# The first RMS norm's tokens laid out feature first: sums through a product with ones, a late chunk, and the S5 parameters on GpSimd

## What is computed

```python
def _rms_norm(x, g):
    y = x * lax.rsqrt(jnp.mean(x * x, axis=-1, keepdims=True) + EPS)
    return y * g

def _prologue(x, ctx, c, c_ctx, g, w_mod, b_mod):
    sh, sc, gt = _ada(c, w_mod, b_mod)            # silu(c) @ w_mod + b_mod, in three parts
    shc, scc, gtc = _ada(c_ctx, w_mod, b_mod)
    hx = _rms_norm(x, g) * (1 + sc[:, None]) + sh[:, None]
    hc = _rms_norm(ctx, g) * (1 + scc) + shc
    return jnp.concatenate([hc, hx], axis=1), ...

def _even_layer(...):
    u, v, g_a, xs, g_b = split(h @ w_in)          # five parts of width 512
    y_a = _chunk_gmlp(u, v, ...) * silu(g_a)      # layer norm of v, 128-token chunks
    y_b = _s5_bidir(xs, lam, log_dt, b, c, ...) * silu(g_b)   # diagonal state space model, both directions
    x = x + gt * (concat(y_a, y_b) @ w_out)

def _s5_discretize(lam_re, lam_im, log_dt, b_re, b_im):
    dt = jnp.exp(log_dt)
    mag = jnp.exp(lam_re * dt)
    lb = mag * (cos(lam_im * dt), sin(lam_im * dt))
    f = (lb - 1) / lam                            # complex; den = lam_re^2 + lam_im^2
    bb = f * b
```

## Time and profile before

| | |
|---|---|
| median of 3 runs | 1305.07 us (1303.98 to 1305.39) |
| profiled execution | 1301.15 us |
| its span, first to last instruction | 1299.3 us |
| mean granted TensorE clock | 0.992 |
| TensorE busy | 1223.0 us, 94% |
| VectorE, ScalarE, GpSimd busy | 851.6, 518.3, 445.6 us |
| HBM read and written | 95.71 and 30.93 MB |

### The profile page before, as it was taken

How to read it: one execution, slowest core, us unless ns; L and a number is a source line. 1 busy time by engine, 2 the same in 40 slices (tenths; PEclk the granted TensorE clock), 3 DMA queues, 4 the chain that set the end, 5 groups by cost and what they waited for, 6 DMA issues and landing times.

```text
span 1299.3 us, 21119 instructions
## 1 busy us (share of the span) xinstructions
PE 1223.0 (94%) x8508; PEld 1079.1 (83%) x8508; DVE 851.6 (66%) x1494; ACT 518.3 (40%) x956; POOL 445.6 (34%) x358
## 2 busy tenths in 40 slices
PE   1799989999999899999999999999999999999997
PEld 1789878888888848999999998877788888888997
DVE  6697956989925253136484899448877877776125
ACT  6632353320015331034524432146666666665012
POOL 0600000000000003332112212139999888988332
PEclk9899999999999999999999999999999999999999
DMA  9614677425422962103211112330000000000402
GB/s 347 241 66 130 153 209 247 148 81 203 162 90 85 324 231 56 64 33 116 70 44 34 33 66 81 111 100 9 9 17 9 17 9 17 17 9 9 162 28 103
DMA packets 87408, 127.99 MB, mean 99 GB/s; under 512 B 12912, under 2 KB 59376, under 8 KB 86512
## 3 DMA queue, kind: packets, MB, share of 16 engines
q1 hardware_dynamic: 77200, 110.81, 25.8%
q10 hardware_dynamic: 10112, 15.85, 3.5%
HBM read 95.71 MB, written 30.93 MB: 97 GB/s over the span
## 4 chain that ended last, share of the span: by engine, by line
PE 78%; DVE 11%; DMA 4%; ACT 3%; POOL 3%; issue 2%; SPq 0%; ACTq 0%; POOLq 0%; DVEq 0%
PE ps L1732 10%; PE ps L1734 10%; PE ps L1733 10%; PE ps L1743 5%; PE ps L1744 5%; PE ps L1745 5%; PE ps L1986 3%; DVE region_d L1008 3%; PE ps L2020 2%; PE ps L2021 2%; PE ps L2022 2%; PE ps L2006 2%; PE ps L2009 2%; PE ps L2008 2%; PE ps L2007 2%; PE ps L1598 2%
## 5 line engine op out<-in xcount | busy, mean ns | idle before, releaser
L1732 PE MATMUL ps<-w_hi,a_hi 128*128 128x256 f32 x896 | 256.6, 286 | 9.9 <-DVE b_lo L1109 6.3
L1733 PE MATMUL ps<-w_lo,a_hi 128*128 128x256 f32 x896 | 254.9, 284 | 0.0
L1734 PE MATMUL ps<-w_hi,c_lo 128*128 128x256 f32 x736 | 208.2, 283 | 0.0
L601 POOL TENSOR_TENSOR region_b<-region_b,region_d 128x256 f32<-128x256 f32 x40 | 29.7, 749 | 510.0 <-DVE region_d L1412 510.0
L1732 PEld LDWEIGHTS ps<-w_hi,a_hi 128*128 128x128 f32 x896 | 173.2, 193 | 12.2 <-issue 3.7
L1733 PEld LDWEIGHTS ps<-w_lo,a_hi 128*128 128x128 f32 x896 | 173.4, 194 | 0.0
L594 POOL TENSOR_TENSOR w_lo<-weight_ring,w_hi 128x2048 fp32r<-128x2048 f32 x16 | 74.0, 4625 | 199.3 <-ACT w_hi L649 199.3
L1734 PEld LDWEIGHTS ps<-w_hi,c_lo 128*128 128x128 f32 x736 | 141.2, 192 | 0.0
L1743 PE MATMUL ps<-a_hi,w_hi 128*128 128x512 f32 (+1 forms) x384 | 138.6, 361 | 1.4 <-ACT region_d L649 1.4
L1508 DVE TENSOR_REDUCE small<-ps 128x1 f32<-128x1280 f32 x64 | 95.2, 1487 | 65.1 <-PE ps L1986 65.1
L1744 PE MATMUL ps<-b_lo,w_hi 128*128 128x512 f32 (+1 forms) x384 | 136.6, 356 | 0.0
(11 more groups left out here) (225 smaller groups left out, 2940.9 us busy)
## 6 DMA issues: line engine op xcount, KB each, us to landing
weight_ring<-in_w_mod SPq DMA_DIRECT2D x10, 2048.0 KB, 8.5
weight_ring<-in_we_in SPq DMA_DIRECT2D x10, 1024.0 KB, 6.0
weight_ring<-in_wo_in SPq DMA_DIRECT2D x10, 1024.0 KB, 5.2
weight_ring<-cop_t_scratch SPq DMA_DIRECT2D x4, 1536.0 KB, 7.9
region_a<-in_x SPq DMA_DIRECT2D x4, 1024.0 KB, 14.4
region_c<-in_w_mod SPq DMA_DIRECT2D x2, 2048.0 KB, 19.3
bop_scratch<-region_d ACTq DMA_DIRECT2D x16, 256.0 KB, 2.6
cop_t_scratch<-region_d SPq DMA_DIRECT2D x8, 512.0 KB, 7.4
```

Source lines behind the costliest of these rows:

```text
L1732: te.matmul(o, th, wh[:, k], start=k == 0, stop=False)
L1733: te.matmul(o, th, wl[:, k], start=False, stop=False)
L1734: last = te.matmul(o, tl, wh[:, k], start=False, stop=k == last_k)
```

## The change

- The host lays the tokens out feature first as well (`xt`). SP loads its first 768 tokens (chunks 0 and 1) in two halves of four slabs into `hT0`. The other 512 (chunk 2) come after the fourth modulation slab, feature first into `hT0` and token first into `XQ`.
- Sums of squares of the first 768: ScalarE squares four slabs in one instruction, VectorE adds two slabs to the other two, TensorE multiplies what is left by a matrix of ones, so each partition has all 768 sums. ScalarE takes 768 roots on every partition, VectorE refines the reciprocals there, and multiplies slabs 0 to 3 by them (`scaled`). Slabs 4 to 7 get it together with their scale (`gained`, `gained_rest`, `gained_round`).
- Chunk 2: ScalarE squares and sums four token tiles, one root, `row_rstd`; TensorE spreads the four columns by transposes (`rstd_across`, listed as "bc" after v tile 1), ScalarE copies them to `rstd_rows`.
- The 80 transposes, their copies and the scalings of tiles are gone. The mods(2) product moves behind v's first two token tiles; weight half 1 of v on slabs 0 to 3 comes ahead of slabs 4 to 7.
- The lists after v and after xs change: bop(4), lags, xs weights, gb weights and vg stand one or two places later. VectorE's evacuation of the sixth modulation slab moves behind build_bl(2), and w_lo of xs ahead of build_cl(0).
- The exponentials, the sine and the signs go from VectorE to GpSimd, in float arithmetic (rounding by adding and subtracting 12582912). VectorE keeps 1 / den.
- The S5 arrays b and c are loaded by SP after the tokens, not by ScalarE at the start.

The orders written out by hand:

```diff
-        early = [(M[0], 0), (M[1], 1), (("v", 0), 2), (("v", 1), 0), (M[4], 1), (M[5], 1), (("xs", 0), 1), (("xs", 1), 0),
+        early = [(M[0], 0), (("v", 0), 2), (M[1], 1), (("v", 1), 0), (M[4], 1), (M[5], 1), (("xs", 0), 1), (("xs", 1), 0),
...
-        after_v = {1: [("mods", 4)], 2: [("cols", 4)], 5: [("mods", 5)], 6: [("cols", 5), ("xs", 0)], 7: [("bop", 0)], 8: [("bop", 4)],
-                   9: [("lags", 0)]}
-        after_xs = {0: [("xs", 1)], 2: [("bop", 8)], 4: [("ws", 0)], 5: [("lags", 1)], 6: [("gb", 0), ("bop", 12)], 7: [("vg", 0)],
-                    8: [("vg", 5)]}
+        after_v = {1: [("bc", 2)], 2: [("mods", 4)], 3: [("cols", 4)], 5: [("mods", 5)], 6: [("cols", 5)], 7: [("xs", 0), ("bop", 0)],
+                   9: [("bop", 4)]}
+        after_xs = {1: [("xs", 1)], 2: [("lags", 0)], 4: [("bop", 8)], 5: [("ws", 0)], 7: [("lags", 1)], 8: [("gb", 0), ("bop", 12)],
+                    9: [("vg", 0)], 10: [("vg", 5)]}
```

SP:

```diff
-            token_loads(X, ld_x)
-            ring_load(*M[0])
-            ring_load(*M[1])
-            ring_load("v", 0)
+            for e in range(2):
+                sp.dma_start(hT0[:, 4 * e:4 * e + 4, 0:T01], xt[:, 4 * e:4 * e + 4, 0:T01]).then_inc(ld_x[e], 16)
+            ring_load(*M[0])
+            ring_load("v", 0)
+            ring_load(*M[1])
+            off_ring_load(2, s_ld_v)
             ring_load("v", 1)
+            off_ring_load(3, s_ld_ws)
+            sp.dma_start(hT0[:, :, T01:TOK], xt[:, :, T01:TOK]).then_inc(ld_x[2], 16)
+            for i in range(4):
+                c = T01 - NCTX + P * i
+                sp.dma_start(XQ[:, 2 * i:2 * i + 2, T01:TOK],
+                             x[0, c:c + P, :].rearrange("p (a f) -> p a f", a=2)).then_inc(ld_x[3 + i // 2], 16)
+            sp.dma_start(braw.rearrange("p r g h -> p (r g h)"), b_in).then_inc(s_ld_b, 16)
+            sp.dma_start(Cx.rearrange("p r g h -> p (r g h)"), c_in).then_inc(s_ld_b, 16)
```

ScalarE:

```diff
+            for e in range(2):
+                act.wait_ge(ld_x[e], 16)
+                a.activation(XQ[:, 4 * e:4 * e + 4, 0:T01], hT0[:, 4 * e:4 * e + 4, 0:T01], ACT.Square).then_inc(s_sq, 1)
+            act.wait_ge(s_ss_mm, 1)
+            act.wait_ge(s_consts, 2)
+            a.activation(rstd_rows[:, 0:T01], sums, ACT.Sqrt, bias=epsc, scale=1.0 / D).then_inc(s_rt, 1)
+            weights_round(("v", 0))
+            mod_row(0)
             mod_row(1)
+            h_round(0)
+            h_round(1)
             mod_row(2)
+            weights_round(("v", 1))
             mod_row(3)
+            gained_round(0, range(4, KT), 0)
+            gained_round(1, range(4, KT), 4)
+            for t in range(6, TT):
+                act.wait_ge(ld_x[t // 2], 32)
+                i = 2 * t - 12
+                z = XQ[:, i:i + 2, T01:TOK]
+                a.activation(z, z, ACT.Square, accum_out=ssq[:, t:t + 1]).then_inc(s_sq, 1)
+            act.wait_ge(s_sq, 6)
+            a.activation(rstd[:, 6:TT], ssq[:, 6:TT], ACT.Sqrt, bias=epsc, scale=1.0 / D).then_inc(s_rt, 1)
+            act.wait_ge(s_bc_mm, 1)
+            copy(rstd_rows[:, T01:TOK], ps[:, 7, :]).then_inc(s_bc_ok, 1)
+            gained_round(2, range(KT), 8)
```

VectorE:

```diff
+            for e in range(2):
+                dve.wait_ge(s_sq, e + 1)
+                z = XQ[:, 4 * e:4 * e + 2, 0:T01]
+                v.tensor_tensor(z, z, XQ[:, 4 * e + 2:4 * e + 4, 0:T01], ALU.add).then_inc(s_pre, 1)
+            dve.wait_ge(s_rt, 1)
+            rows = rstd_rows[:, 0:T01]
+            ts(rows_m, sums, 1.0 / D, ALU.mult, EPS, ALU.add)
+            refined(rows_t, rows_m, rows)
+            scaled(0)
+            scaled(1)
+            weights_rest(("v", 0))
             half_evac(0)
+            h_rest(0)
+            h_rest(1)
+            weights_rest(("v", 1))
             half_evac(1)
+            gained(0, range(4, KT))
+            gained_rest(0, range(4, KT), 8)
+            gained(1, range(4, KT))
+            gained_rest(1, range(4, KT), 12)
+            dve.wait_ge(s_rt, 2)
+            row_rstd(slice(6, TT))
+            v.tensor_copy(small[:, 335:336], small[:, 0:1]).then_inc(s_rs0, 1)
+            dve.wait_ge(s_bc_ok, 1)
+            for e in range(2):
+                gained(2, range(4 * e, 4 * e + 4))
+                gained_rest(2, range(4 * e, 4 * e + 4), 16 + 4 * e)
...
             build_bl(1)
-            mod_evac(0, 6, 16, 24)
+            weights_rest(("xs", 0))
             build_cl(0)
-            weights_rest(("xs", 0))
...
             weights_rest(("xs", 1))
+            mod_evac(0, 6, 16, 24)
             k_diagonal(0)
```

TensorE:

```diff
+            def rstd_across():
+
+                pe.wait_ge(s_rs0, 1)
+                pe.wait_ge(s_mod_ev, 2)
+                for i in range(4):
+                    last = tr(ps[:, 7, P * i:P * i + P], rstd[:, 6 + i:7 + i].broadcast_to([P, P]))
+                last.then_inc(s_bc_mm, 1)
+
+            for e in range(2):
+                pe.wait_ge(s_pre, e + 1)
+                for k in range(4 * e, 4 * e + 2):
+                    te.matmul(sums[:, 0:256], ones_f, XQ[:, k, 0:256], start=k == 0, stop=k == 5)
+                    last = te.matmul(sums[:, 256:T01], ones_f, XQ[:, k, 256:T01], start=k == 0, stop=k == 5)
+            last.then_inc(s_ss_mm, 1)
             mods(0)
             mod_cols(0)
-            to_features(0, *x0)
             mods(1)
             mod_cols(1)
-            to_features(1, *x0)
-            mods(2)
-            mod_cols(2)
...
+            ws = [split_of(("v", 0))]
             for t in range(6):
                 if t == 2:
-                    to_features(2, *x0)
+                    mods(2)
+                    mod_cols(2)
+                for k in range(4):
+                    if t in (0, 2):
+                        pe.wait_ge(s_h_lod, k + 1 if t == 0 else k + 5)
+                    v_part(ws[0], t, 0, (k,))
+            ws.append(split_of(("v", 1)))
+            for t in range(6):
+                if t == 2:
                     mods(3)
+                if t == 3:
                     mod_cols(3)
+                v_part(ws[1], t, 1, range(4))
             for t in range(TT):
+                if t in (0, 2, 6):
+                    pe.wait_ge(s_h_lod, {0: 12, 2: 16, 6: 24}[t])
                 if t >= 6:
                     pe.wait_ge(s_v_ev, t - 5 if t < 8 else t - 1)
+                ks = range(4 if t < 6 else 0, KT)
+                v_part(ws[0], t, 0, ks)
+                v_part(ws[1], t, 1, ks).then_inc(s_v_mm, 1)
                 between_tiles(after_v.get(t, ()))
```

302 lines of the change are left out of this document (134 added, 168 removed).

## The result

The changed kernel takes 1309.01 us (median of 6, 1307.67 to 1311.44), the kernel before beside it 1304.13: a ratio of 1.0041, 95% interval 1.0026 to 1.0055. Timed again on another chip it was 1.0036 (1.0021 to 1.0050). It is slower by some 5 us, where the forecast was 1304.1 and the range ended at 1309.0. The profiled execution took 1309.46, its span is 1307.7, 8.4 more than before's. Two further profiles of the kernel before (one with an input that nobody reads) have spans of 1302.4 and 1301.9, so its first was a short one; three further ones of the changed kernel (one with its inputs in another order) have 1304.0, 1302.9 and 1301.9, so its first was a long one.

The account below looks back on a forecast made before the run. TensorE, busy 94%, was taken to bound the kernel. Its first product comes 8.6 us earlier, but S 5.7 later delays CL(1) and ScalarE sets gating at 203.2 against 204.20: -1.0 us, 1304.1, range 1297 to 1309.

Parts of the forecast that it names:

- What bounds: Whole kernel: TensorE, busy 94% of a 1299.3 us span, so a change in front pays only where TensorE still waits.
- the new front: Start to the first product with tokens: TensorE starts it at 40.4, not 48.99, 8.6 us earlier.
- The v stage: TensorE waits 4.2 us for the late chunk's rstd, yet is through v at 118.8, some 8 us earlier.
- S: End of VectorE's work on h, ahead of its first BB pass: 85.8 against 80.08, 5.7 us later.
- 16 passes of 0.62: VectorE's last passes on h, after the late chunk's transposes and copy: 16 at 0.62 us each, ending at S.
- Where that goes: Chain after v: CL(0) at 126.2 (before 124.6), xs1 landing at 142.4, CL(1) at 167.8 (before 164.6).
- Behind lags(1): ScalarE has more work than TensorE there and sets the gating products: 203.2 against 204.20.
- Behind 204.20 every wait is relative and the code is the same: After the gating products: nothing changes, so what is gained or lost there, 1.0 us gained, holds at the end.
- (1): Chain behind S does not bind and TensorE keeps its 8 us: 1297; chance 0.30.
- (2): TensorE's clock stays low in the ones product and first v tiles: S = 90.8, a loss of 4.0, 1309; chance 0.13.
- (3): GpSimd's steps outlast S: 1306.5 if they end at 88.2, 1311 at 93.1; chance 0.09.
- (4): Front isn't shorter, 768 roots costing VectorE what 80 transposes cost TensorE: first product at 49, S 94.4, 1312.7; chance 0.08.

Follow-up runs that it names:

- pe_pad: Changed kernel with 138 more TensorE instructions at its start that only look at a semaphore long set: 0.9990 of the kernel before.
- squares_early: Changed kernel with the late chunk's squares, root, row_rstd and transposes moved earlier, into idle time: 0.9997 of the kernel before.
- xs1_early: Changed kernel with SyncE asking for the second xs slab ahead of CL(0)'s stores: 1.0014 of the kernel before.
- xt_last: Changed kernel with the new input declared behind all other inputs, no instruction changed: 1096.7 us behind gating.
- kd1_first: Changed kernel with k_diagonal(1) ahead of w_lo of the first gb slab on VectorE: 1.0025 of the kernel before.
- before: The kernel before, unchanged, first profile: gating products at 204.2 and 1095.1 us behind them, span 1299.3.
- after_again: The changed kernel, unchanged, profiled a second time: gating products at 206.1 and 1097.9 us behind them.
- before_again: The kernel before, unchanged, profiled a second time: gating products at 207.1 and 1095.3 us behind them.
- sq_all_pad: Changed kernel with four orders moved together (late squares, xs1, k_diagonal(1), u_in(2)) and 138 do-nothing TensorE instructions at the start: 0.9954 of the kernel before.
- before_xt: The kernel before with the new input declared but read by nobody: gating products at 205.3 and 1096.6 us behind them.
- the four orders: Changed kernel with late squares in front, xs1 ahead of CL(0)'s stores, k_diagonal(1) ahead of gb's w_lo, u_in(2) behind the last evacuation: 0.9942 of the kernel before.
- the padded changed kernels: Changed kernel with 138 or 64 do-nothing TensorE instructions at its start: 0.9990 and 0.9995 of the kernel before.

## Why the prediction was wrong

**What bounds, and the new front: right.** The second half landed at 13.3, where the sum had 12.2 and the bound 13, squares 2.76 (2.8), ones product to 22.2 (20.5), root by 23.2 (22.7), reciprocal 4.95 (4.8), first v product 40.72 (40.4). A pair of 512 columns of the ones product took TensorE 1.91 us up to 19.3 and 1.02 in the last 2.8, much as the sum had it; but the granted clock is 1.00 over both (14.1 to 22.1), so the rows don't show this as the lower level, and the kernel before's 3.60 for its first slab stands under 1.00 as well. Two steps were wrong and cost nothing. The reciprocal's rows (353 ns for 32, 253 for 16) give 6.25 ns an element and not 6.1, and 4.95 us for 768, which is what it took. And the table load (16.10) runs ahead of the root's wait, so the 1.28 that was added is hidden.

**The v stage: right in kind, S mis-sized.** mod_cols(3) 61.6 (60.3), row_rstd to 74.9 (74.6), TensorE's wait 3.35 (4.2). S is 88.4 and not 85.8: "16 passes of 0.62" took 11.7. Twelve of them took 0.68; the first four 0.95, and beside these GpSimd ran four copies (76.17 to 80.01, timeline of GpSimd). In pe_pad, where the copies were done at 79.26 and the passes began at 78.80, the first four took 0.75. By the Trainium skill (GPSIMD Engine Reference, Specifications) the two engines contend for SBUF interfaces when a VectorE instruction has two SBUF inputs, as these have; the trace agrees. The price, 0.27 a pass on VectorE's side, was counted only on GpSimd's.

**Where that goes: the chain right, with one wait too few.** CL(0) came at 130.4 (126.2): 2.6 of S and 2.25 of a wait that the sum had not: w_lo of xs stands ahead of build_cl(0) and ScalarE rounds xs0 only behind its evacuation of tile 7. CL(1) 170.7 (167.8), TensorE's wait for it 1.4 (1.5). squares_early and xs1_early moved the chain from its two ends, and CL(1) followed by 5.2 and 2.9.

**Behind lags(1).** ScalarE was late as said: bop evacuations 186.3 (184.8), u_in(2) 203.8 (202.0), gating 204.9 (203.2). "Two issues 1.3" took 3.35; the four bop evacuations 4.8, not 6.5. Not seen: VectorE stands 6.8 us for gb's rounding with k_diagonal(1) queued behind it, which moved the stores of K to 189.5 to 205.0 and beside bop and the last store of xs.

**The step that failed: "Behind 204.20 every wait is relative and the code is the same, so what is gained or lost there is gained or lost at the end."** Measured on several profiles, the part up to the gating products is even: 205.5 (mean of 204.9, 206.1, 205.8 and xt_last's 205.3) against 205.5 (204.2, 207.1, 205.3), where the forecast had a gain of 1.0. Behind them it is a mean of 1098.6 against 1095.7: 2.9 us in a place that the sum put at nothing. TensorE's waits there give about that: 1.4 against 0.4 at the modulation slab, 4.0 against 2.7 at the c products (the late out slab), 0.8 against none at bop. The instructions are the same, their places in the code packets are not. The 1.0 of the modulation slab stands in every profile of the changed kernel, and was made to appear in the kernel before by padding alone. That the packets also make the out slab late is argued from the comparison above, and bop's wait goes with late stores of K (kd1_first, with early ones, has none). The prediction named the bop load as a place that could break the sum and gave it no term. The sum was also made against one profile, the fastest of three.

**A reading that no run tests: the clock.** By the table of stretches in steps of 10 us (a granted clock under 1.00 counted as time at the lower level, 0.50), TensorE stood at the lower level behind the gating products for 10.2, 13.6, 6.8 and 13.6 us in the four profiles of the changed kernel, and for 3.4, 3.4 and 13.6 in the three of the kernel before, mostly 240 to 280 us behind them, in the c and y stages. From before, 444.20 to 454.20, and after_again, 446.13 to 456.13 (length, TensorE busy, granted clock, DMA share, GB/s):

```profile
444.20:454.20 10.00, 7.29 (x57) 1.00 0.97 346
...
446.13:456.13 10.00, 7.21 (x29) 0.57 0.84 303
```

At half speed the mean difference, 4.3 us, costs up to 2.1. The four profiles with 3.4 us at the lower level (before, before_again, pe_pad, sq_all_pad) are also the four shortest behind gating, 1095.1 to 1095.6; but before_xt took only 1096.6 with 13.6. Whether the clock is a cause of its own or follows the longer waits is open.

**The rivals.** (1) fell: the chain bound. (2) the clock: 0.84 in 40.7 to 60; S was 88.4 where it wanted 90.8, so a part of its loss at most. (3) GpSimd ended at 82.7, where the sum had 66.6 and 19 us of cover, and didn't bind; it did at 85.5 once S was to fall below. (4) fell, 40.72.

**What stays open.** The miss is the gain of 1.0 that isn't there, 2.9 behind gating, and 1.8 to 2.4 more between the medians (4.7 to 5.3) that no mean of profiles has. The changed kernel's timed executions spread over 1304.7 to 1312.7, the padded one's over 1301.1 to 1304.1, and no profile shows where the longer ones lose the rest. That padding gave all 5 us back is measured; that code packets are all of its effect is not shown. On the kernel before and on the four orders it gave nothing, and the padded changed kernels also have a higher mean granted clock in their timed executions (0.986 and 0.984 against 0.981 and 0.982; the kernel before 0.989).

## What to carry to other kernels

A head start on TensorE is worth what the slowest queue behind it lets through: before counting it, follow the first order that waits (here a late chunk's root, then SyncE's store ahead of a load, then VectorE's w_lo ahead of what SyncE stores) and move that; three such moves turned +0.4% into -0.5%, some of which may be where the packets fell. Make the sum against several profiles. And when instructions leave the front of a long program, look again at transfers and dense code behind it. Padding that does nothing moved one of these kernels by 6 us and two others not at all, so try a padded twin before judging an edit of that size.

## What the runs showed of the hardware

- TensorE's code arrives during the run, 67 packets of 16 KB. With one of them or of q14's in the transfer of a 2 MB slab, loaded alone, TensorE started on it 9.5 to 9.9 us behind the issue instead of 8.7 to 8.8 (17 profiles against 3). The pages have 252 TensorE records a packet (8448 products and as many weight loads over 67). By the Trainium skill (Perfetto Trace Analysis, The 4-stage abstract model) an instruction has 64 bytes, by which 16 KB hold an estimated 256. The records come near it, though waits are not among them and some fp32 products show two.
- In a stretch of short products a packet goes with 1.4 to 2.9 us of TensorE's own "issue" wait (14 profiles; none in the six without a packet there).
- A reciprocal of 768 elements took 4.95 us, 6.4 ns an element; four scalar-tensor-tensor passes of 512 took 3.80 beside GpSimd's copies and 2.72 without.
- TensorE's products can take twice as long under a granted clock of 1.00: a pair of 512 columns 1.91 us in the changed kernel's first work (to 19.3) and 1.02 right behind it.
